# Reading a chunk's 512 tokens in crossed pieces of 32 in the split-weight matmuls of a two-block transformer kernel

## What is computed

```python
proj = h @ w_in[l]
h = layer_norm(DEEPNORM_ALPHA * h + mixed @ w_out[l], ln1_g[l], ln1_b[l])
ff = jnp.square(jax.nn.relu(h @ w_up[l])) @ w_down[l]
...
gate, up = jnp.split(x @ wi, 2, axis=-1)
return (jax.nn.silu(gate) * up) @ wo
```

## Time and profile before

| what | us |
|---|---|
| median of three runs | 3432.18 |
| lowest and highest | 3431.13, 3433.72 |
| the profiled execution | 3430.66 |
| its span, first to last instruction | 3428.8 |
| TensorE busy in the span | 3317.4 |
| VectorE, ScalarE, GpSimd busy | 1836.8, 1241.6, 342.3 |

### The profile page before, as it was taken

The page is one execution under the profiler, slowest core; times in us unless marked ns, Lnnn a source line. Parts: engine busy times, 40 slices in busy tenths (PEclk is TensorE's granted clock), DMA queues, the critical chain, the costliest instruction groups (busy, mean ns, idle before and its releaser), DMA issues.

```text
span 3428.8 us, 42531 instructions
## 1 busy us (share of the span) xinstructions
PE 3317.4 (97%) x16570; PEld 2633.9 (77%) x16570; DVE 1836.8 (54%) x2932; ACT 1241.6 (36%) x1878; POOL 342.3 (10%) x244
## 2 busy tenths in 40 slices
PE   9999999999899999999999999999999989999997
PEld 6667888776688887888777778887788876688886
DVE  5776334567752446443566664435644357654436
ACT  3354222424442324332333342324432235532324
POOL 0310000212100020000233100000000012100001
PEclk9999999999999999999999999999999999999999
DMA  4102222311122222223322122232222321122232
GB/s 162 62 32 74 96 95 98 128 62 50 50 85 94 98 98 81 98 97 104 107 74 68 63 81 96 98 105 93 86 96 94 105 94 39 61 98 98 98 105 80
DMA packets 81431, 300.35 MB, mean 88 GB/s; under 512 B 9040, under 2 KB 9040, under 8 KB 80640
## 3 DMA queue, kind: packets, MB, share of 16 engines
q1 hardware_dynamic: 78624, 284.20, 24.8%
q0 software_dynamic: 1568, 11.98, 0.9%
q10 hardware_dynamic: 1088, 2.10, 0.2%
HBM read 296.14 MB, written 2.10 MB: 87 GB/s over the span
## 4 chain that ended last, share of the span: by engine, by line
PE 88%; DVE 6%; ACT 3%; issue 1%; POOL 1%; DMA 1%; ACTq 0%; DVEq 0%; POOLq 0%
PE bank L874 25%; PE bank L876 25%; PE bank L875 24%; PE bank L918 2%; PE bank L925 2%; PE bank L919 2%; DVE wl L2026 1%; PE bank L1411 1%; ACT sc L1710 1%; PE bank L1423 1%; PE bank L1175 1%; PE bank L1156 1%; ACT wh L1549 1%; PE bank L1466 1%; PE bank L1114 1%
## 5 line engine op out<-in xcount | busy, mean ns | idle before, releaser
L874 PE MATMUL bank<-x,wh 128*128 128x512 f32 x2632 | 1053.7, 400 | 14.8 <-DVE h L2470 5.7
L876 PE MATMUL bank<-x,wl 128*128 128x512 f32 x2632 | 1027.3, 390 | 0.0
L875 PE MATMUL bank<-x,wh 128*128 128x512 f32 x2632 | 1026.1, 390 | 0.0
L1549 ACT ACTIVATE wh<-raw 128x1024 fp32r<-128x1024 f32 x528 | 558.0, 1057 | 1171.6 <-PE bank L876 1083.6
L2026 DVE TENSOR_TENSOR wl<-raw,wh 128x1024 fp32r<-128x1024 f32 x528 | 677.7, 1284 | 567.4 <-ACT wh L1549 566.0
L874 PEld LDWEIGHTS bank<-x,wh 128*128 128x128 f32 x2632 | 494.9, 188 | 135.9 <-issue 29.4
L876 PEld LDWEIGHTS bank<-x,wl 128*128 128x128 f32 x2632 | 494.6, 188 | 105.4
L875 PEld LDWEIGHTS bank<-x,wh 128*128 128x128 f32 x2632 | 495.7, 188 | 98.4 <-issue 3.4
L874 PE MATMUL bank<-mid,wh 128*128 128x512 f32 x1216 | 474.9, 391 | 0.5 <-DVE wl L2026 0.5
L876 PE MATMUL bank<-mid,wl 128*128 128x512 f32 x1216 | 473.1, 389 | 0.0
L875 PE MATMUL bank<-mid,wh 128*128 128x512 f32 x1216 | 473.1, 389 | 0.0
(11 more groups left out here) (340 smaller groups left out, 3294.5 us busy)
## 6 DMA issues: line engine op xcount, KB each, us to landing
raw<-stream SPq DMA_DIRECT2D x528, 512.0 KB, 3.3
raw_apart<-stream SPq DMA_DIRECT2D x10, 512.0 KB, 3.6
sm<-small POOLq DMA_DIRECT2D x2, 2144.0 KB, 10.6
tb<-tab POOLq DMA_DIRECT2D x2, 1728.0 KB, 14.8
h<-x_t ACTq DMA_DIRECT2D x4, 512.0 KB, 6.8
out_t<-h SPq DMA_DIRECT2D x8, 256.0 KB, 2.1
tba<-tab_a POOLq DMA_DIRECT2D x1, 1152.0 KB, 8.5
pf<-p_t POOLq DMA_DIRECT2D x2, 512.0 KB, 3.9
```

What stands on the lines that cost most here:

```text
L874: pe.matmul(dst, hi, src[:, kc, 0, :], start=start, stop=False)
L875: pe.matmul(dst, hi, src[:, kc, 1, :], start=False, stop=False)
L876: return pe.matmul(dst, lo, src[:, kc, 0, :], start=False, stop=stop)
L1549: act.activation(high_of(n)[:, :], raw_of(n)[:, :], ACT.Copy).then_inc(hi_done, 1)
```

## The change

The tokens of a chunk are no longer read from 0 to 511. `crossed` splits them into two halves of 256 tokens (`b`), each of eight runs (`a`) of 32 tokens (`c`), and orders them by `a`, then `b`, then `c`: tokens 0 to 31, 256 to 287, 32 to 63, 288 to 319, and so on. The output in PSUM is written in the same order, so each token's result lies where it lay. All matmuls of `piece` and `abreast` are changed so, and no other instruction; their number, operands, waits and order stay. A run of 32 tokens is 128 bytes; a half chunk is 1024 bytes, so runs 0 and 256 lie in the same half of a 256-byte period and runs 32 and 288 in the other.

```diff
+RUN = 32
...
+            def crossed(ap):
+
+
+                return ap.rearrange("p (b a c) -> p a b c", b=2, c=RUN)
+
             def piece(dst, u, col, src, kc, start, stop):
 
                 hi, lo = high_of(u)[:, col:col + P], low_of(u)[:, col:col + P]
-                pe.matmul(dst, hi, src[:, kc, 0, :], start=start, stop=False)
-                pe.matmul(dst, hi, src[:, kc, 1, :], start=False, stop=False)
-                return pe.matmul(dst, lo, src[:, kc, 0, :], start=False, stop=stop)
+                dst, x_hi_, x_lo_ = crossed(dst), crossed(src[:, kc, 0, :]), crossed(src[:, kc, 1, :])
+                pe.matmul(dst, hi, x_hi_, start=start, stop=False)
+                pe.matmul(dst, hi, x_lo_, start=False, stop=False)
+                return pe.matmul(dst, lo, x_hi_, start=False, stop=stop)
...
                 dst = bank[c.homes[t][0]][:, :]
-                pe.matmul(dst, hi, x[:, kc, 0, :], start=kc == 0, stop=False)
-                pe.matmul(dst, lo, x[:, kc, 0, :], start=False, stop=False)
+                pe.matmul(crossed(dst), hi, crossed(x[:, kc, 0, :]), start=kc == 0, stop=False)
+                pe.matmul(crossed(dst), lo, crossed(x[:, kc, 0, :]), start=False, stop=False)
                 if t < width - 1:
                     return
                 c.wait(x_ready)
                 for i in range(width):
                     dst, hi = bank[c.homes[i][0]][:, :], high_of(u + i)[:, at_]
-                    mm = pe.matmul(dst, hi, x[:, kc, 1, :], start=False, stop=kc == 7)
+                    mm = pe.matmul(crossed(dst), hi, crossed(x[:, kc, 1, :]), start=False, stop=kc == 7)
```

## The result

The changed kernel takes **3539.1 us** (median of four runs, 3538.75 to 3540.11) against 3431.65 us for the kernel before beside it: a ratio of **1.0313**, 95% interval 1.0295 to 1.0331. It is slower by 107 us, where 115 us less were forecast. The profiled execution took 3540.1 us, with a span of 3538.3.

What follows compares the result with a forecast made beforehand. The prediction took TensorE's dense matmul step as the bound: 100.7 us saved outside the mixers plus 14.4 us in them, 115 us; 3430.7 - 115 + 1.5 = 3317 us, range 3290 to 3590.

Steps and rivals of the forecast that it cites:

- What bounds the kernel: Whole kernel: how fast TensorE's dense matmuls follow each other sets the end, 226.7 ns a step, TensorE busy 97%.
- Jumps cost nothing: Dense matmuls' access pattern, 15 jumps each: taken as nothing, at most 13.3 ns a matmul.
- The excess of 13.3 ns is the two reads meeting: Full-clock dense step: 13.3 ns over 213.3, from weight load and moving operand meeting in one half half of the time.
- part (3): Dense matmuls: excess goes from 13.3 ns to between 0 and 26.7, taken as 3.2, so 10.2 ns less a step.
- The step of 0.24 us: Dense matmul behind a pause: 26.7 ns over 213.3, read as load and moving operand meeting all the time.
- 216.5 ns: Forecast settled step of a dense matmul after the change, 10.2 ns less than 226.7.
- The argument that the streams slide to where they meet least: Steps behind a pause fall from 0.24 us to 226.7 ns; new order gives the streams a place without meetings.
- The mixers: 118 units, 2,832 matmuls: half the gain counted, 14.4 us, since dense matmuls there often fill a softmax's time.
- The one that ended slower: Rival: load and moving operand begin in the same half and always meet; 240 ns a step, 3582 us, chance 0.27.
- No change: Rival: the order is nothing to the excess; step stays 226.7 ns, time 3432 us, chance 0.15.
- a part of the gain: Rival: the reads still meet a third to nearly half the time; steps 221 to 225 ns, 3365 to 3410 us, chance 0.12.
- The rival from the Trainium skill: TensorE's read ports for moving operand and weights are independent, so nothing meets; 3432 us, no chance of its own.

Runs made afterwards that it cites:

- L93: Block of 40 like matmuls alone, moving operand in runs of 32 tokens starting 384 bytes apart, halves by turns, against straight order: 226.7 ns a step.
- L92: Block of 40 like matmuls alone in the same block kernel, moving operand read without a jump: 226.7 ns a step.

## Why the prediction was wrong

- **What bounds the kernel** was right. TensorE's step is the time: 10.0 ns more in it made 107 us more.
- **No instruction added, no other queue touched** was right: the other engines' busy time is the same to 3 us.
- **Jumps cost nothing** was right, and now is shown for runs of 128 bytes: L93 against L92, 226.7 ns both. Runs of 64 in the kernel, with seven jumps, are at 0.9997. The upper bound of 13.3 ns was far too wide.
- **The excess of 13.3 ns is the two reads meeting** is the step that failed, part (3). The forecast took the load of weights for the other party, let it stay in a half for 27 ns, and drew from it that two moving pieces in each half could slip past it. The runs show another thing in its place: at full clock it counts where neighbouring 128-byte pieces of the moving operand lie. With the same load, the step is 226.7 ns when they lie in different halves of 256 bytes and 236.7 when they lie in the same one, or two by two. A load of one column leaves the crossed step at 236.7, and moving the weights to the other half leaves the changed kernel at 3540.6 us. The change took what the straight order does well, turning to the other half behind each 128 bytes, and did it half as often. The halves were right; who meets in them was not. How the 10.0 ns divide is not shown: with one column of weights 5.6 ns of them are left (236.7 against 231.1), with the weights 128 bytes off in the kernel 4.3 (236.7 against 232.4). The rest goes with the load: straight order gains it with a full load at the common place, and crossed order doesn't. The step of 0.24 us, read as "always meeting", suggested the load because its start and the matmul's coincide, but rows that coincide in every matmul can't tell a cause from a companion. It was one step, too: the eight behind it in the same rows take 224 to 236 ns.
- **216.5 ns** was mis-sized with it (and 3 / 27 of 26.7 is 3.0, not 3.2). The floor of 213.3 ns from half of the half-clock step is not reached by any order tried. The Trainium skill's 215.8 ns (TensorE: Matmul & The Clock Gate, Back-to-back issue gap) is what the bfloat16 blocks measured to the tenth; for float32r the best is 226.7. The forecast used it for a stream, but in the same section the Trainium skill gives that formula for an isolated matmul and about 131 ns for 512 columns in a stream with its loads. No block of 512 columns comes near that, in either type.
- **The argument that the streams slide to where they meet least** was wrong as a reason for a gain. Crossed order settles too, but into a cycle of four steps, 233, 236, 237 and 241 ns. It does so at once behind a pause, which the forecast took for a sign of a place without meetings.
- **The mixers**: half of the effect was counted there, 60% came (6.0 of 10.0 ns a matmul). The stretch from 350 to 610 us holds 1100 matmuls, where about 1200 were forecast and 1149 stood before. The count was a little high as well: 9,870 x 10.0 and 2,832 x 6.0 ns make 116 us, and 107 came.
- **The rivals.** The one that ended slower said 240 ns and 3582 us; 236.7 ns and 3539 us came. Its sign was right, its step nearly so, its mechanism wrong: it put the decision on which half the load begins in, and moving the load changed nothing. No change (3432 us) and a part of the gain (3365 to 3410) are excluded by the measured time. The rival from the Trainium skill (SBUF — State Buffer, Who interferes with whom), independent ports for the moving operand and the weights, had the time stay at 3432 us, and the measurements speak against it in part: with all reads in one half the load's own half is worth 4.4 ns of 240.0, and the place of the weights makes 61 us in straight order. The runs don't show whether the ports are where the two reads meet.

Left open: why two pieces in a row in a half cost 10.0 ns, four 6.7, eight and sixteen 10.0, and two in another phase 6.7; what the straight order's own excess of 13.3 ns is, which is nearly the same from 256 to 512 columns and is 2.5 ns in bfloat16; and how the place of the weights enters, since a narrower load makes straight order slower (231.1 ns with one column), not faster.

## What to carry to other kernels

A sweep through memory that looks wasteful in the trace may already be the best order: before reordering a dense stream, price the order by itself, in a block of forty like matmuls with nothing beside them, and vary each party alone (the load's width, its place, the input's order, the output's). For float32r matmuls at full clock, read the moving operand so that neighbouring pieces of 128 bytes lie in different halves of 256 bytes, with runs of 64 tokens or more, each from the same place in 256 bytes, where a permuted order is needed, and let it begin at the same place in 256 bytes as the weights: the first was worth 3.1%, the second, against a place 128 bytes off, 1.8% of this kernel. Try other places in a block first, since a few others reach the same step. A coincidence of starts in the trace names a suspect, not a cause.

## What the runs showed that was not expected

- The place of the weights against the moving operand, in straight order: 226.7 ns at 0, 256, 512, 1024 and 4096 bytes of difference, 228.9 at 64 and 320, 230 to 235 at most others, 236.7 at 4 and 116 bytes. But 226.7 stands also at 108 bytes, at 112 in one of two blocks, and with the weights moved by 496. In the kernel 128 bytes cost 1.8%.
- Fewer weights make straight order slower: 128 columns 226.7 ns, 96 and 64 230.0, 32 231.7, 16 and 1 231.1.
- Reading every second token (a step of 8 bytes) takes 453.3 ns for 512 columns, twice the straight step; pieces of two tokens from each 32nd take 473.
- The straight order's excess over 2.4 GHz is 13.3 ns at 256, 320, 384 and 512 columns alike (120.0, 146.7, 173.3, 226.7), and 16.0 at 448 (202.7).
- The order in which a matmul writes a bank in PSUM, in runs of 128 bytes, costs nothing (226.7).
